# Four of eight samples' value pages summed on GpSimd instead of TensorE, in one layer of a hybrid decoder

## The chip, the cores and the metric

The kernel runs on one core of a Trainium2 chip. The metric is the device time of one execution in microseconds, taken as the median over runs. A core has TensorE (PE, matrix products into PSUM), VectorE (DVE), ScalarE (ACT) and GpSimd (POOL) for elementwise work, and SyncE (SP), which here only starts DMAs. The engines run side by side, each through its own list of instructions in order, and wait for each other at semaphores.

## What is computed

One layer of a decoder, for 256 tokens of a prompt and 8 samples with one new token each: a normalised input goes through one wide projection, then through an attention branch and a Mamba-2 (SSD) branch, both gated, merged, projected, and followed by a gated FFN. Cut to what matters here:

```python
h = rmsnorm(x, norm_mix_pre)
q, k, v, z, xbc, dt_raw, g_attn, g_ssm = split(h @ w_in)
attn = moba_attention(q, k_all, v_all, q_pos0)    # prompt: own keys; a sample: 1024 past keys and values
ssm, conv_new, ssm_new = mamba2_branch(z, xbc, dt_raw, ...)
merged = sigmoid(g_attn) * (attn @ w_attn_out) + sigmoid(g_ssm) * (ssm @ w_ssm_out)
x = x + rmsnorm(merged @ w_out, norm_mix_post)
x = x + rmsnorm(swiglu(rmsnorm(x, norm_ffn_pre), w_gate, w_up, w_down), norm_ffn_post)

# attention of one sample, for each of 16 heads of 64 numbers; p is 0 in the blocks left out
p = softmax(q . k_past / 8 over the chosen 3 of 4 blocks, and the own key)
out = sum over 1024 positions of p * v_past, + p_own * v
```

The past keys and values lie in pages of 128 positions x 1024 numbers (512 KB), found by a page table: eight pages of keys and eight of values for each sample.

## The kernel before

All is fp32. Weights are split into a high part (w_hi, made by ScalarE's `hi_half`) and the rest (w_lo, made by VectorE's `lo_half`: raw minus w_hi), and each product is taken as three fast ones. The work is cut into 562 *blocks*: one block is 128 output columns by up to eight 128-row slices of a weight, 24 matmuls on TensorE over all 264 tokens. w_hi lies in a ring of four, so ScalarE and VectorE can be up to three blocks ahead of TensorE. The blocks come in the fixed order of `pairs`: projection (blocks 0 to 209), SSM output (210 to 241), attention output (242 to 257), and so on.

All other work stands beside the blocks by hand. Each engine runs `for b in range(END)`: its share of block b, and then `side_work(b)`, in which tables of block numbers say what is due. SyncE starts what stands at b when TensorE begins block b (`wait(sp, mm_done, b)`), and its list is in order too. ScalarE issues the weight loads.

The samples' attention has two parts. *Keys* (block 30 on, `K_AT`): SyncE loads a page of keys into one of four slots of `kv`, GpSimd multiplies it with the query (line 744), VectorE sums over each head (line 1401). After the softmax (`SEL`, done at block 150; GpSimd's list then holds only `ends`), *values* (`V_AT`, blocks 152 to 232): for each of four pairs of samples there are eight steps, one page of each of the two samples at a time, two blocks apart (`VG[w] + 2 g`). A step (lines 2017 to 2029) is four fp32 products of 32 columns of probabilities with half a page, each in two passes, side by side in four column groups of TensorE; all heads are multiplied with all columns, and the eight steps add up in the PSUM bank `side[3]`. VectorE then keeps each head's own columns (`vm_done`, line 1461), TensorE adds these up (the *pair sum*, line 2034, four products in two passes each), and VectorE adds the own token into `attn` (line 1468). A step uses two of the four slots and its loads are issued four blocks ahead.

In the same blocks the SSD groups run (`SSD`: a group every eleven blocks; GpSimd's `ends` makes its `xw`, which TensorE needs at `SSD[g] + 6` and + 7; TensorE writes `y` to `side[0]` at + 10), the old states of the samples are read (`STATE`; `st`, `stx`, `crows`), and `u` is normalised (`UN`, blocks 196 to 214). ScalarE writes the gates `gate_a`, 16 tiles of 264 columns, from `ga` pairs, the last four pairs at blocks 201 to 213. `side[0]` and `side[2]` are PSUM banks that these share.

## Time and profile before

| | us |
|---|---|
| median of 3 runs | 1783.56 (1782.84 to 1790.49) |
| profiled execution, its own time | 1781.87 |
| its span | 1780.1 |
| TensorE busy | 1756.1 |
| VectorE busy | 1193.5 |
| ScalarE busy | 912.5 |
| GpSimd busy | 221.1 |

TensorE's granted clock is full (1.00) in all the stretches that are spoken of here. "Busy" is the time in which an engine works on an instruction; where it is held up inside an instruction by another engine, that counts as busy too, and the instruction's duration grows. A matmul row shows a duration of about 0.28 us, but matmuls overlap: what one costs is the distance between the starts of neighbours.

In the value stage the trace finds these starts of value steps: block 152 at 519.8 us, 174 at 603.3, 188 at 657.5, 196 at 685.4, 210 at 740.4, 218 at 766.1, 232 at 815.1.

### The profile page before, as it was taken

To read this page: it belongs to the slowest core of one execution; us is meant where nothing else is said; L and a number is where in the kernel's file an instruction comes from. 1 tells how busy PE (TensorE), PEld (TensorE's weight loads), DVE (VectorE), ACT (ScalarE), POOL (GpSimd) and SP (SyncE) were. 2 spreads that over 40 slices of the span, in tenths; PEclk is the share of its full clock that TensorE was granted. 3 is DMA by queue.
4 is the path that set the end of the run, shared out by engine and by line. 5 is a ranking of instruction groups with operands and counts; after the bars stand their busy time and mean duration, and the time that the engine had idled before them with its cause. 6 is when DMAs were issued, how large, how long until landed. Compare 5 with 4: busy or idle time off the path is not lost.

```text
span 1780.1 us, 35190 instructions
## 1 busy us (share of the span) xinstructions
PE 1756.1 (99%) x14510; PEld 1708.2 (96%) x14510; DVE 1193.5 (67%) x1679; ACT 912.5 (51%) x1724; POOL 221.1 (12%) x127
## 2 busy tenths in 40 slices
PE   8999999999999999999999999999999999999997
PEld 7999999999988988889999999999999999999997
DVE  6468999999887656845755666666666666444444
ACT  5544556555766556533454655554555454434442
POOL 2144645564000000000000000000000000000000
PEclk9999999999999999999999999999999999999999
DMA  8589988897789999695565487777777776655553
GB/s 256 174 271 332 321 269 275 281 305 243 229 266 338 291 306 328 223 304 189 186 222 182 134 276 228 223 227 234 219 226 235 217 235 202 215 177 189 164 181 97
DMA packets 398272, 421.39 MB, mean 237 GB/s; under 512 B 13040, under 2 KB 375984, under 8 KB 397072
## 3 DMA queue, kind: packets, MB, share of 16 engines
q10 hardware_dynamic: 284480, 285.62, 49.9%
q1 hardware_dynamic: 113280, 132.85, 23.0%
q8 instruction: 114, 1.87, 0.4%
q0 software_dynamic: 352, 0.67, 0.2%
q14 instruction: 46, 0.38, 0.1%
HBM read 400.70 MB, written 18.66 MB: 236 GB/s over the span
## 4 chain that ended last, share of the span: by engine, by line
PE 91%; DVE 6%; DMA 1%; ACT 1%; SPq 0%; issue 0%; DVEq 0%; ACTq 0%
PE gemm L1770 29%; PE gemm L1771 28%; PE gemm L1772 28%; DVE w_lo L1204 2%; PE side L2026 2%; PE side L1732 1%; DVE sc_flat L1401 1%; DMA kv<-in_cache_v 1%; DMA xtok<-in_x_prompt 1%; DVE u L1196 0%; DVE conv_out L1196 0%; DVE un L1524 0%; ACT w_hi L774 0%; DVE dec L1193 0%; PE side L1922 0%
## 5 line engine op out<-in xcount | busy, mean ns | idle before, releaser
L1204 DVE TENSOR_TENSOR w_lo<-raw,w_hi 128x1024 fp32r<-128x1024 f32 (+1 forms) x562 | 737.9, 1317 | 538.6 <-ACT w_hi L774 537.7
L1770 PE MATMUL gemm<-x_hi,w_hi 128*128 128x264 f32 x3312 | 951.7, 287 | 3.7 <-DVE x_lo L1532 1.9
L1772 PE MATMUL gemm<-x_hi,w_lo 128*128 128x264 f32 x3312 | 938.2, 283 | 0.0
L1771 PE MATMUL gemm<-x_lo,w_hi 128*128 128x264 f32 x3312 | 937.9, 283 | 0.0
L774 ACT ACTIVATE w_hi<-raw 128x1024 fp32r<-128x1024 f32 (+1 forms) x562 | 585.6, 1044 | 655.3 <-PE gemm L1772 654.8
L1770 PEld LDWEIGHTS gemm<-x_hi,w_hi 128*128 128x128 f32 x3312 | 623.6, 188 | 30.9 <-issue 24.1
L1771 PEld LDWEIGHTS gemm<-x_lo,w_hi 128*128 128x128 f32 x3312 | 624.4, 189 | 0.9 <-issue 0.5
L1772 PEld LDWEIGHTS gemm<-x_hi,w_lo 128*128 128x128 f32 x3312 | 621.1, 188 | 0.0
L744 POOL TENSOR_TENSOR kv<-kv,qb 128x1024 f32<-128x1024 f32 x64 | 180.6, 2830 | 176.4 <-DMA kv<-in_cache_k 176.3
L1771 PE MATMUL gemm<-g_lo,w_hi 128*128 128x264 f32 x704 | 200.4, 285 | 0.0
L1770 PE MATMUL gemm<-g_hi,w_hi 128*128 128x264 f32 x704 | 199.9, 284 | 0.0
L1772 PE MATMUL gemm<-g_hi,w_lo 128*128 128x264 f32 x704 | 199.6, 284 | 0.0
L1770 PEld LDWEIGHTS gemm<-g_hi,w_hi 128*128 128x128 f32 x704 | 132.6, 188 | 0.0
L1772 PEld LDWEIGHTS gemm<-g_hi,w_lo 128*128 128x128 f32 x704 | 132.6, 188 | 0.0
L1771 PEld LDWEIGHTS gemm<-g_lo,w_hi 128*128 128x128 f32 x704 | 132.2, 188 | 0.0
L1401 DVE TENSOR_REDUCE sc_flat<-kv 128x16 f32<-128x1024 f32 x64 | 77.2, 1207 | 2.3 <-POOL kv L744 2.3
L1770 PE MATMUL gemm<-m_hi,w_hi 128*128 128x264 f32 x256 | 73.3, 286 | 0.0
L1771 PE MATMUL gemm<-m_lo,w_hi 128*128 128x264 f32 x256 | 72.5, 283 | 0.0
L1772 PE MATMUL gemm<-m_hi,w_lo 128*128 128x264 f32 x256 | 72.5, 283 | 0.0
L774 ACT ACTIVATE stx<-stx 128x128 f32<-128x128 f32 x128 | 37.8, 299 | 31.1 <-DVE stx L1193 31.1
L1770 PEld LDWEIGHTS gemm<-m_hi,w_hi 128*128 128x128 f32 x256 | 48.2, 188 | 0.1
L1771 PEld LDWEIGHTS gemm<-m_lo,w_hi 128*128 128x128 f32 x256 | 48.3, 189 | 0.0
(324 smaller groups left out, 1391.9 us busy)
## 6 DMA issues: line engine op xcount, KB each, us to landing
raw<-in_w_in ACTq DMA_DIRECT2D x99, 1024.0 KB, 7.3
raw<-in_w_gate ACTq DMA_DIRECT2D x44, 1024.0 KB, 5.2
raw<-in_w_up ACTq DMA_DIRECT2D x44, 1024.0 KB, 5.7
raw<-in_w_down ACTq DMA_DIRECT2D x40, 1024.0 KB, 5.4
kv<-in_cache_k SPq DMA_DIRECT2D x64, 512.0 KB, 5.8
kv<-in_cache_v SPq DMA_DIRECT2D x64, 512.0 KB, 6.1
st<-in_state_ssm SPq DMA_DIRECT2D x64, 256.0 KB, 5.5
raw<-in_w_ssm_out ACTq DMA_DIRECT2D x16, 1024.0 KB, 7.3
```

Of the source, the lines that this page charges most:

```text
L744: gp.tensor_tensor(out=page_slot(m), in0=page_slot(m), in1=qb[:, n % 2, :], op=ALU.mult)\
L774: return nc.scalar.activation(out, in_, f, **kw)
L1204: v.tensor_tensor(w_lo[:, s, 0:blk.kts, cols], raw[:, s, 0:blk.kts, cols], w_hi[:, b % RING, 0:blk.kts].bitcast(fp32), ALU.subtract).then_ ...
L1401: v.tensor_reduce(out=sc[:, g, n, :], in_=by_head(page_slot(m)), axis=AX.X, op=ALU.add)\
L1732: return nc.tensor.transpose(out, in_, ident[0:k, 0:k])
L1770: mm(out, w_hi[:, b % RING, k], pr.hi[:, x], start=(x == 0), stop=False)
L1771: mm(out, w_hi[:, b % RING, k], pr.lo[:, x], start=False, stop=False)
L1772: ins = mm(out, w_lo[:, s, k, cols], pr.hi[:, x], start=False, stop=(x == pr.kt - 1))
L2026: ins = mm(side[3][32 * n:32 * n + 32, :], sc_flat[:, first_col:first_col + 32], page_slot(2 * m + e)[:, half * 512:(half + 1) * 512], sta ...
```

## The change

Samples 0 to 3 (two pairs) stay with TensorE, in steps that are now four blocks apart (`VE`: 153 to 181, and 188 to 216) and use slots 0 and 1 alone. Samples 4 to 7 go to GpSimd: every two blocks from 149 to 211 (`PV_AT`) SyncE loads one value page into slot 2 or 3, and two blocks later GpSimd multiplies it in place with its probabilities, spread over each head's 64 columns, and adds it to `vsum`; a sample's first page is multiplied straight into `vsum`. For each sample TensorE then sums `vsum` over the 128 positions by eight products with a column of ones (the *page sum*, `PV_SUM`: blocks 174, 186, 211 and 221, in `side[0]` or `side[2]`), and VectorE adds the own token. `vsum` takes the place of gate tiles 8 to 15, which are now written over the old states' buffers (`gate_b`, `gate_c`), once all 32 state multiplications are done. GpSimd's `ends` stand three blocks earlier. The load of the page table is counted with the other small vectors (`vecs_in` for `pages_in`, left out below). Where `v_cp` was waited for up to 4 it is now 6, or the count of the sum whose bank is used next (left out too, but for one).

```diff
@@ -165,6 +165,9 @@
+        gate_b = at("gate_b", [P, 7, T], fp32, T0)
+        gate_c = at("gate_c", [P, T], fp32, T0 + 9984)
+        vsum = at("vsum", [P, 2, AW], fp32, G0 + 8704)
...
-        VG = [152 + 22 * w for w in range(4)]
+        VE = [[153 + 4 * g for g in range(NPG)], [188 + 4 * g for g in range(NPG)]]
+        PV_AT = [149 + 2 * q for q in range(4 * NPG)]
+        PV_SUM = [174, 186, 211, 221]
+        PAIR_NTH, SUM_NTH = [2, 5], [1, 3, 4, 6]
+        V_ALL = 6
-        V_AT = [VG[w] + 2 * g for w in range(4) for g in range(NPG)]
+        V_AT = [x for two in VE for x in two]
...
+        def pooled_page(q):
+            return kv[:, 2 + q % 2, :]
+        def gate_a_of(t):
+            return gate_a[:, t, :] if t < 8 else gate_b[:, t - 8, :] if t < 15 else gate_c[:, :]
+        def sum_psum(j):
+            return side[(0, 0, 2, 0)[j]][:, 0:2 * AT]
...
-                for m in range(4 * NPG):
-                    if b != V_AT[m] - 4:
+                for m in range(2 * NPG):
+                    if b != V_AT[m] - 3:
-                    if m == 0:
-                        sp.wait_ge(k_red, NB * NPG)
-                    wait(sp, v_mm, m - 1)
-                    if g < 2:
-                        wait(sp, vs_mm, w)
+                    wait(sp, v_mm, m)
+                    if g == 0:
+                        wait(sp, vs_mm, PAIR_NTH[0] if w else 0)
-                        sp.dma_start(page_slot(2 * m + e), src).then_inc(kv_in[m % 2], 16)
+                        sp.dma_start(kv[:, e, :], src).then_inc(kv_in[0], 16)
+            def pooled_loads(b):
+                for q in range(4 * NPG):
+                    if b != PV_AT[q]:
+                        continue
+                    if q == 0:
+                        sp.wait_ge(k_red, NB * NPG)
+                    wait(sp, pg_add, q - 1)
+                    src = vc[bass.ds(page_of(4 + q // NPG, q % NPG), 1)].rearrange("g p n -> p (g n)")
+                    sp.dma_start(pooled_page(q), src).then_inc(kv_in[2 + q % 2], 16)
...
-                    if d == 5:
+                    if d == 2:
...
-                    if d == 6:
+                    if d == 3:
+            def pooled_values(b):
+                for q in range(4 * NPG):
+                    if b != PV_AT[q] + 2:
+                        continue
+                    j, g = q // NPG, q % NPG
+                    page, total = pooled_page(q), vsum[:, j % 2, :]
+                    share = sc[:, g, 4 + j, :].unsqueeze(2).to_broadcast([P, HEADS, HD])
+                    if q == 0:
+                        gp.wait_ge(p_done, 1)
+                    if g == 0 and j >= 2:
+                        gp.wait_ge(vs_mm, SUM_NTH[j - 2])
+                    gp.wait_ge(kv_in[2 + q % 2], 256 + 16 * (q // 2 + 1))
+                    if g == 0:
+                        gp.tensor_tensor(out=by_head(total), in0=by_head(page), in1=share, op=ALU.mult)\
+                            .then_inc(pg_add, 1)
+                    else:
+                        drained(gp.tensor_tensor(out=by_head(page), in0=by_head(page), in1=share, op=ALU.mult))
+                        gp.wait_ge(pg_add, q)
+                        gp.tensor_tensor(out=total, in0=total, in1=page, op=ALU.add).then_inc(pg_add, 1)
+                pooled_values(b)
...
-                        func(gate_a[:, t, :], ps[:, 0:T], ACT.Tanh, scale=0.5).then_inc(free_out[par], 1)
+                        if t >= 8:
+                            act.wait_ge(st_mul, 4 * NB)
+                        func(gate_a_of(t), ps[:, 0:T], ACT.Tanh, scale=0.5).then_inc(free_out[par], 1)
...
-                for w in range(4):
-                    if b == VG[w] + 18:
+                for w in range(2):
+                    if b == VE[w][-1] + 4:
-                        mul(by_head(kv[:, 2, 0:512]), by_head(side[3][:, :]), own).then_inc(vm_done, 1)
-                    if b == VG[w] + 21:
-                        dve.wait_ge(vs_mm, w + 1)
+                        mul(by_head(kv[:, 0, 0:512]), by_head(side[3][:, :]), own).then_inc(vm_done, 1)
+                    if b == VE[w][-1] + 7:
+                        dve.wait_ge(vs_mm, PAIR_NTH[w])
...
+                for j in range(4):
+                    if b == PV_SUM[j] + 4:
+                        dve.wait_ge(vs_mm, SUM_NTH[j])
+                        n = 4 + j
+                        v.tensor_tensor(attn[:, :, TP + n], sum_psum(j)[:, 0:2 * AT:2],
+                                        own_t[:, n * AT:(n + 1) * AT], ALU.add).then_inc(v_cp, 1)
...
+                        for j in range(2):
+                            if PV_SUM[j] < b <= PV_SUM[j] + 11:
+                                pe.wait_ge(v_cp, SUM_NTH[j])
...
-                for m in range(4 * NPG):
+                for m in range(2 * NPG):
-                        wait(pe, v_cp, w)
-                    pe.wait_ge(kv_in[m % 2], 256 + 32 * (m // 2 + 1))
+                        wait(pe, v_cp, PAIR_NTH[0] if w else 0)
+                    pe.wait_ge(kv_in[0], 256 + 32 * (m + 1))
-                                 page_slot(2 * m + e)[:, half * 512:(half + 1) * 512],
+                                 kv[:, e, half * 512:(half + 1) * 512],
-                for w in range(4):
-                    if b == VG[w] + 17:
+                for w in range(2):
+                    if b == VE[w][-1] + 3:
-                            ins = mm(side[3][:, 4 * k:4 * k + 4], kv[:, 2, k * P:(k + 1) * P], bsel[:, :],
+                            ins = mm(side[3][:, 4 * k:4 * k + 4], kv[:, 0, k * P:(k + 1) * P], bsel[:, :],
+                                     start=True, stop=True)
+                        ins.then_inc(vs_mm, 1)
+                for j in range(4):
+                    if b == PV_SUM[j]:
+                        pe.wait_ge(pg_add, NPG * (j + 1))
+                        if j < 2:
+                            pe.wait_ge(y_done, 6 + j)
+                        if j == 2:
+                            pe.wait_ge(un_sd, 6)
+                        if j == 3:
+                            pe.wait_ge(ct_cp, 3)
+                        for t in range(AT):
+                            ins = mm(sum_psum(j)[:, 2 * t:2 * t + 2], vsum[:, j % 2, t * P:(t + 1) * P], ones[:, 0:2],
...
```


The order of GpSimd's list, where the SSD groups 6 and 7 lay alone (blocks 176 to 188); each three rows are one group's `xw`:

```order
L756 TENSOR_TENSOR xw_86<-xdt,dend 128x256
L759 TENSOR_TENSOR xw<-xw_86,cdec 128x256
L764 TENSOR_TENSOR xw_86<-xdt,dend 128x256
L756 TENSOR_TENSOR xw_86<-xdt,dend 128x256
L759 TENSOR_TENSOR xw<-xw_86,cdec 128x256
L764 TENSOR_TENSOR xw_86<-xdt,dend 128x256
L58 UNCONDITIONAL_BRANCH
```

The same engine now, from block 171 to block 175:

```order
L812 TENSOR_TENSOR kv<-kv,sc_flat 128x1024
L814 TENSOR_TENSOR vsum<-vsum,kv 128x1024
L784 TENSOR_TENSOR xw_86<-xdt,dend 128x256
L787 TENSOR_TENSOR xw<-xw_86,cdec 128x256
L812 TENSOR_TENSOR kv<-kv,sc_flat 128x1024
L814 TENSOR_TENSOR vsum<-vsum,kv 128x1024
L792 TENSOR_TENSOR xw_86<-xdt,dend 128x256
L812 TENSOR_TENSOR kv<-kv,sc_flat 128x1024
L814 TENSOR_TENSOR vsum<-vsum,kv 128x1024
```

Two large operations for a page now stand before, between and behind those of a group.

TensorE's side work in blocks 152 to 158, without the large matmuls between the rows (first before, then now); `kv,sc_flat` is a value step, the others belong to an SSD group:

```order
L2026 MATMUL side<-kv,sc_flat 32x512 x4
...
L2026 MATMUL side<-kv,sc_flat 32x512 x4
...
L1960 MATMUL side<-bct 128x128 x2
L1961 MATMUL side<-xw_86,btok 128x256
...
L1966 MATMUL side<-btok,xw 128x128
L1967 MATMUL side<-btok,xw_86 128x128
L1966 MATMUL side<-btok,xw 128x128
L1967 MATMUL side<-btok,xw_86 128x128
L2026 MATMUL side<-kv,sc_flat 32x512 x4
...
L2026 MATMUL side<-kv,sc_flat 32x512 x4
```

```order
L2087 MATMUL side<-kv,sc_flat 32x512 x4
...
L2018 MATMUL side<-bct 128x128 x2
L2019 MATMUL side<-xw_86,btok 128x256
...
L2024 MATMUL side<-btok,xw 128x128
L2025 MATMUL side<-btok,xw_86 128x128
L2024 MATMUL side<-btok,xw 128x128
L2025 MATMUL side<-btok,xw_86 128x128
...
L2087 MATMUL side<-kv,sc_flat 32x512 x4
```

Four steps have become two, the rest keeps its place.

## Rows read from the trace of the kernel before

**Rows 1.** The page: busy time by engine, and the chain's shares.
```profile
PE 1756.1 (99%) x14510; PEld 1708.2 (96%) x14510; DVE 1193.5 (67%) x1679; ACT 912.5 (51%) x1724; POOL 221.1 (12%) x127
...
PE 91%; DVE 6%; DMA 1%; ACT 1%; SPq 0%; issue 0%; DVEq 0%; ACTq 0%
```

**Rows 2.** Waits of TensorE, whole run: us, times, longest.
```profile
PE gemm L1770 <- DVE x_lo L1532: 1.9, 2, 1.2
...
PE side L2026 <- DMA kv<-in_cache_v: 0.5, 1, 0.5
```

**Rows 3.** Timeline of TensorE around one value step: start, duration.
```profile
772.89 0.28 PE L1772 MATMUL gemm<-x_hi,w_lo 128*128 128x264 f32 x1
773.10 1.06 PE L2026 MATMUL side<-kv,sc_flat 128*32 128x512 f32 x8
774.09 0.39 PE L1770 MATMUL gemm<-x_hi,w_hi 128*128 128x264 f32 x1
774.32 0.28 PE L1771 MATMUL gemm<-x_lo,w_hi 128*128 128x264 f32 x1
```

**Rows 4.** Timeline of TensorE around one pair sum.
```profile
585.17 0.28 PE L1772 MATMUL gemm<-x_hi,w_lo 128*128 128x264 f32 x1
585.29 0.95 PE L2034 MATMUL side<-bsel,kv 128*128 128x4 f32 x8
586.09 0.37 PE L1770 MATMUL gemm<-x_hi,w_hi 128*128 128x264 f32 x1
586.30 0.28 PE L1771 MATMUL gemm<-x_lo,w_hi 128*128 128x264 f32 x1
```

**Rows 5.** Windows: stretch, length, busy PE, PEld, DVE, ACT, POOL, clock, DMA.
```profile
100.00:440.00 340.00, 338.92 (x2857) 331.33 (x2857) 317.30 (x360) 182.82 (x374) 188.06 (x70) 1.00 0.89 292
514.00:758.00 244.00, 241.59 (x1979) 215.42 (x1978) 165.78 (x274) 152.80 (x408) 10.97 (x12) 1.00 0.92 303
```

**Rows 6.** GpSimd's line 744, durations in ns: min/median/max.
```profile
L744 POOL TENSOR_TENSOR kv<-kv,qb x64: 2377/2586/3739, 102.7 to 430.6; 128x1024 f32<-128x1024 f32 x64
```

**Rows 7.** Timeline of GpSimd, 400 to 405 us.
```profile
400.23 0.61 POOL L759 TENSOR_TENSOR xw<-xw,cdec 128x256 f32<-128x256 f32 x1
400.80 2.41 POOL L744 TENSOR_TENSOR kv<-kv,qb 128x1024 f32<-128x1024 f32 x1
403.16 1.60 POOL L764 TENSOR_TENSOR xw<-xdt,dend 128x256 f32<-128x256 f32 x1
```

**Rows 8.** Timeline of VectorE at the same time.
```profile
401.06 3.23 DVE L1204 TENSOR_TENSOR w_lo<-raw,w_hi 128x1024 fp32r<-128x1024 f32 x1
```

**Rows 9.** Groups of VectorE, 100 to 440 us: busy us, mean ns.
```profile
L1204 DVE TENSOR_TENSOR w_lo<-raw,w_hi 128x1024 fp32r<-128x1024 f32 x103 | 184.2, 1797 | 21.8 <-ACT w_hi L774 21.5
L1401 DVE TENSOR_REDUCE sc_flat<-kv 128x16 f32<-128x1024 f32 x63 | 76.0, 1207 | 2.3 <-POOL kv L744 2.3
```

**Rows 10.** Groups of VectorE, 514 to 758 us.
```profile
L1204 DVE TENSOR_TENSOR w_lo<-raw,w_hi 128x1024 fp32r<-128x1024 f32 x66 | 81.1, 1229 | 75.2 <-ACT w_hi L774 75.2
L1193 DVE TENSOR_TENSOR stx<-st,crows 128x512 f32<-128x512 f32 x22 | 15.0, 684 | 0.0
...
L1196 DVE SCALAR_TENSOR_TENSOR u<-u,gains,un 128x264 f32<-128x264 f32 x16 | 7.2, 491 | 0.3
L1532 DVE TENSOR_TENSOR x_lo<-u,x_hi 128x264 fp32r<-128x264 f32 x16 | 5.8, 425 | 0.0
L1193 DVE TENSOR_TENSOR dec<-dec,cbm 128x512 f32<-128x512 f32 x8 | 5.2, 688 | 0.1
...
L1196 DVE SCALAR_TENSOR_TENSOR u<-tmp,u 128x256 f32<-128x256 f32 x10 | 4.2, 418 | 0.0
...
L1510 DVE TENSOR_TENSOR ysam<-ysam,both_t 128x32 f32<-128x32 f32 x3 | 0.6, 192 | 0.1
```

**Rows 11.** DMA issues, 514 to 758 us: KB each, median us to landing.
```profile
kv<-in_cache_v SPq DMA_DIRECT2D x48, 512.0 KB, 6.3
...
crows<-bc_row SPq DMA_DIRECT2D x20, 128.0 KB, 9.5
```

More of the change, by code:

```diff
@@ L638, in side_work @@
                 key_loads(b)
+                pooled_loads(b)
                 value_loads(b)
@@ L875, in time_steps @@
                 if b == DT + 2:
-                    act.wait_ge(vecs_in, 48)
+                    act.wait_ge(vecs_in, 64)
                     p = at_pair["dt", 0]
@@ L1034, in attn_halves @@
                 if b == B_AO - 2:
-                    act.wait_ge(v_cp, 4)
+                    act.wait_ge(v_cp, V_ALL)
                     act.wait_ge(u_lo, KT)
@@ L1627, in evac @@
                         t = 2 * i + n
-                        gate = gate_s if pr.kind == "so" else gate_a
+                        gate = gate_s[:, t, :] if pr.kind == "so" else gate_a_of(t)
                         if t == 0 and pr.kind == "so":
@@ L1631, in evac @@
                         dve.wait_ge(mm_done, last_of[p][n] + 1)
-                        stt(gate[:, t, :], gate[:, t, :], 1.0, gemm_ps[2 * par + n][:, 0:T], ALU.add, ALU.mult)\
+                        stt(gate, gate, 1.0, gemm_ps[2 * par + n][:, 0:T], ALU.add, ALU.mult)\
                             .then_inc(free_out[par], 1)
@@ L1637, in evac @@
                         dve.wait_ge(free_out[par], freed(p) - 1 + n)
-                        v.tensor_tensor(gate_s[:, t, :], gate_s[:, t, :], gate_a[:, t, :], ALU.add).then_inc(ao_sum, 1)
+                        v.tensor_tensor(gate_s[:, t, :], gate_s[:, t, :], gate_a_of(t), ALU.add).then_inc(ao_sum, 1)
                     for n in range(2):
@@ L2043, in u_norm @@
                         pe.wait_ge(fin_cp, NG)
+                        pe.wait_ge(v_cp, SUM_NTH[1])
                         wait(pe, un_sd, g - 2)
@@ L2051, in conv_tails @@
                     pe.wait_ge(un_sd, NG)
+                    pe.wait_ge(v_cp, SUM_NTH[2])
                     pe.wait_ge(xbc_done, CT)
@@ L2063, in token_sums @@
                     pe.wait_ge(ct_cp, 3)
-                    pe.wait_ge(v_cp, 4)
+                    pe.wait_ge(v_cp, V_ALL)
                 if i == 7:
```

16 lines of the change are left out of this document (8 added, 8 removed).

## The prediction

> **What bounds the kernel now.** I read the engine shares and the chain of waits first. TensorE is busy 99% of the span and 91% of the chain is its own work [rows 1]; what it waits for is small, 1.9 us for VectorE's x_lo and 0.5 us for a value page [rows 2]. So a pass taken off TensorE is worth its whole time, as long as the engine behind it keeps up. Every block (one 128-column weight tile over eight 128-row slices, 24 matmuls 0.12 us apart, 2.9 us) needs a w_lo from VectorE. Second, I read VectorE where GpSimd also works. In the key stage (100 to 440 us) VectorE is busy 317 of 340 us with GpSimd at 188, in the value stage (514 to 758 us) 166 of 244 with GpSimd at 11 [rows 5]. That stretch is blocks 151 to 215, over which the change spreads its GpSimd pages.
>
> **What the change takes off TensorE.** A value step (eight passes over two pages) is read against the matmuls around it: from the last before it to the second after it 1.43 us [rows 3], where two steps of 0.12 would stand, so 1.19 us. It drops 16 of 32: 19.0 us. A pair sum is 585.17 to 586.30 less the same two steps, 0.89 us [rows 4], and two of four go: 1.8 us. The one wait for a page, 0.5 us, goes with it [rows 2]. Added are four page sums, each 8 fp32 products of 128x128 weights with 2 columns, so 16 passes. The trace has no such row; the nearest is the pair sum, same weights, 4 columns, 8 passes in 0.80 us, so 0.89 + 0.80 = 1.69 us each, 6.8 in all. Bounds: 4.4 for all if only the 0.12 us between large matmuls and half as many passes counted, 9 if each needed 0.14. TensorE's own balance: -19.0 - 1.8 - 0.5 + 6.8 = **-14.5 us**, of which -7.9 lies in blocks 151 to 215 (24 steps become 15, three pair sums become one, three page sums come) and -6.6 behind (8 steps become 1, one page sum comes). This needs nothing else to become late.
>
> **What it puts on GpSimd.** 32 pages: four start a sum (one multiply), 28 take a multiply and an add, so 60 operations of 128x1024. The nearest row is the key multiply: 2.38 us at its least, 2.59 in the median [rows 6]. The broadcast operand costs nothing extra by the 128x256 xw row with one, 0.61 us for a quarter of the size [rows 7]. I take 2.39 where nothing holds it: 143 us, and with the twelve xw operations already there (12 x 0.61 = 7) 151 us, to go into a stretch that TensorE would now pass in 244 - 7.9 = 236 us. Alone it fits.
>
> **What it does to VectorE.** This is the step that decides. The w_lo subtraction takes 1.23 us in the mean of the value stage but 1.80 in the key stage, while the reduction of a page, which has one input, keeps 1.21 there [rows 9, 10]. The timeline says why: w_lo started at 401.06, GpSimd's multiply ran from 400.80 to 403.21, and w_lo ended at 404.29, 1.08 us after it; GpSimd's xw of 403.16 then took 1.60 for 0.61, ending 0.61 after w_lo's end at about 404.2. So the two take turns, whole instructions at a time [rows 7, 8]. Instructions with one SBUF input (the reduction, the steps that read PSUM) run beside GpSimd.
>
> The Trainium skill says the same in "SBUF — State Buffer", section "SBUF: two separate sides": the port pair is an exclusive lock, kept for the instruction by whichever starts first, against a VectorE instruction with two SBUF inputs, and the other blocks fully. The trace agrees, with the 3.23 us w_lo above. If the two merely shared bandwidth, this change would keep its gain.
>
> So in blocks 151 to 215 turns must add up. VectorE's two-input work there is w_lo 81.1, stx 15.0, u 7.2, x_lo 5.8, dec 5.2, and 17 of smaller forms, u from tmp (4.2) the largest and ysam (0.6) among the last [rows 10]: 132 us in 176 instructions, less about 0.08 us each by which a row overlaps the next, 118 us. With GpSimd's 151 that is 269 us of turns for 236 us of TensorE. Key stage, same count: 64 x 2.39 + 4 = 157 and, with some 14 for the smaller forms, 103 x 1.13 + 14 = 130, 287 of 340, which fitted, and TensorE lost 1 us there [rows 5]. The value stage would be at 114%.
>
> Ends of the cost, for that stretch against today's 244 us:
> - least: turns packed without a gap, less the lead of two blocks (2 x 2.9 = 6 us) that the weight ring allows: 263, +19. If GpSimd may also finish as late as its last sum (block 221) instead of 215, six more blocks (17 us of TensorE for some 8 us of VectorE's turns) relieve it by up to 9: +10.
> - most: nothing of VectorE beside GpSimd: 166 + 151 - 6 = 311, +67.
> - by the key stage: GpSimd's 157 us there cost VectorE about 103 x 0.57 = 59 on w_lo and, as an estimate in the ratio 14 to 116 of the turns, 9 more on the smaller forms, 68 in all, so 89 ran beside the 142 us (340 - 68 - 130) in which VectorE was idle or on one-input work, 62%. Here that is 166 - 118 = 48 us, 30 of it covered: 166 + 151 - 30 - 6 = 281, +37.
> I take +28, the middle of +19 and +37, and with the -6.6 behind the stretch **+21 us**. The saving inside the stretch is then worth nothing, since w_lo and not TensorE sets the pace.
>
> **The moved and added waits.** SyncE issues page q at block 149 + 2q, behind a wait for page q - 2's add; queued behind it are the state rows, the decay rows and TensorE's pages. A page lands in 6.3 us and the state's crows take 9.5 [rows 11]. A slot's round is 6.3 + 1.5 to issue + two operations with one turn of VectorE each, 7 or so, 15 us for four blocks; four blocks are 14 us at TensorE's pace and 16 at the slower one, so SyncE runs at most a block late. The last V loads come three blocks ahead instead of four and no longer wait for the step just before: cost nothing, 0.5 per step if late. xw stands three blocks earlier in GpSimd's list, where it blocks the pages until VectorE's xdt is there: it delays a page by about a block, covered by the slack of sum 0 (page 7 done at block 167, used at 174), less so for sum 1 (183, used at 186). A late sum 1 costs up to 8 us; I put 0 in. The last gate tiles wait for the last state multiply, one block before them on VectorE; ScalarE is two blocks ahead: nothing, 2 us if VectorE lags. The merged semaphore costs nothing, since all four small loads are long done.
>
> **Sum.** The profiled execution took 1781.87 us, span 1780.1 and 1.8 around it. 1781.9 + 21 = **1803 us**. It lies 1.7 below the median of the runs, 1783.56, well inside their spread.
>
> **Rivals.**
> 1. *Absorbed by slack, faster.* VectorE is idle in 78 of 244 us of the value stage, and in the key stage it took 93% load with TensorE losing 1 us [rows 5]. If the turns cost only 68/157 of GpSimd's time as there, VectorE needs 166 + 65 = 231 of 236 us and nothing waits: 1781.9 - 14.5 = 1767. Against it: the 86 us of GpSimd that would have to run beside VectorE's one-input and idle time find only 48 + 5.
> 2. *GpSimd is the one that gives way.* Turns go mostly to VectorE and pages pile up to the last sum at block 221. Then the least case holds with +10 - 6.6: 1785. Against it: SyncE would be held behind page adds, and state rows with it.
> 3. *Queue jam.* GpSimd falls over a block behind, SyncE stands in a page's wait, crows and V pages come late, and TensorE waits for the sums as well. From +37, plus 8 for sum 1 and some 10 for late rows: 1830. This decides from a page round of over four blocks (16 us).
>
> **Chances.** Main case 0.58 (own range 1790 to 1818), rival 1 0.17, rival 2 0.15, rival 3 0.10. A measurement here tells about 0.5%, 9 us, from no change. Faster: rival 1 and a little, 0.19. Same: most of rival 2 and the foot of the main case, 0.20. Slower: 0.61. The range leaves most of rival 1 outside below and the far part of the most-case above: 1774 to 1832.
>
> **What would show it.** Right: w_lo's mean in blocks 151 to 215 rises to 1.8 us or more with its median of other stages unchanged, and TensorE's waits in the stretch are for w_lo, some 25 to 35 us. The stretch of the value stage grows, the stages behind 830 us keep their length. Page sums show 16 passes in about 1.7 us. Wrong: TensorE as full as today there and the span 14 us shorter (rival 1); waits of TensorE on vsum or kv instead of w_lo (rivals 2, 3); GpSimd's page operations far off 2.4 to 3.2 us each.

## The result, and the profile after

| | before | after |
|---|---|---|
| median, us (lowest to highest) | 1786.78 (1782.84 to 1790.49) | 1822.88 (1819.80 to 1829.95) |
| profiled execution / its span | 1781.87 / 1780.1 | 1829.95 / 1828.4 |

The ratio is 1.0203, with a 95% interval of 1.0181 to 1.0224. The change makes the kernel 36 us slower. The forecast was 1803, 16 above the same median, with a range that ended at 1832: the direction came out and so did the turns of the two engines, the size did not.

First the page of the changed kernel, against [rows 1]: busy time by engine, then VectorE's, GpSimd's and the granted clock's lines over 40 equal slices.

```profile
PE 1765.4 (97%) x14430; PEld 1728.8 (95%) x14430; DVE 1305.0 (71%) x1677; ACT 909.4 (50%) x1724; POOL 365.5 (20%) x187
...
DVE  6468999999899999974665666666666666444444
...
POOL 2155544455027576420000000000000000000000
PEclk8999999999999999889999999999999999999999
```

TensorE has 80 matmuls fewer and is busy for 9 us *more*. That can't come from waiting; it is the first sign of something that the prediction left out. VectorE has two instructions fewer and is busy for 111 us more.

The windows of TensorE locate it. Columns: stretch, length, busy (instructions), granted clock, DMA share, GB/s. The four stretches are the start, up to block 149 (the own token's scores, `own_p`), blocks 149 to 214 (the transposes of `tails`), and the rest. Before:

```profile
0.00:370.00 370.00, 362.30 (x3007) 1.00 0.85 274
370.00:510.60 140.60, 138.33 (x1171) 1.00 0.78 242
510.60:754.00 243.40, 240.96 (x1973) 1.00 0.92 301
754.00:1780.00 1026.00, 1014.52 (x8365) 1.00 0.65 207
```

After, at the same places of the program:

```profile
0.00:370.00 370.00, 362.70 (x2985) 0.99 0.83 271
370.00:524.80 154.80, 146.72 (x1194) 0.96 0.74 225
524.80:809.00 284.20, 248.10 (x1934) 0.93 0.86 285
809.00:1828.40 1019.40, 1007.93 (x8324) 1.00 0.63 201
```

So the 48.3 us between the two profiled spans (12 more than between the medians, for the profiled execution of the changed kernel is its longest, and that of the kernel before is among its shortest) divide like this:

| stretch | length | idle TensorE (length less busy) | busy TensorE |
|---|---|---|---|
| up to block 149 | +14.2 | +5.4 | +8.8 |
| blocks 149 to 214 | +40.8 | +33.7 | +7.1 (39 matmuls fewer, clock 0.93 for 1.00) |
| behind | -6.6 | 0.0 | -6.6 |

The third row is the -6.6 us that was forecast for it. The second was put at +28, the first at nothing. What TensorE waits for (us in total, times, longest), against [rows 2]:

```profile
PE gemm L1828 <- DVE w_lo L1256: 18.4, 11, 5.2
PE gemm L1828 <- DVE x_lo L1590: 9.4, 1, 9.4
PE side L2121 <- DVE u_sq L1579: 8.7, 4, 5.0
PE side L2087 <- DMA kv<-in_cache_v: 4.8, 3, 3.1
...
PE side L2039 <- DVE dec L1245: 2.6, 2, 1.6
```

All but the pages' 4.8 us is VectorE being late. Its groups from 514 to 758 us, against [rows 10]: busy us, mean ns of one.

```profile
L1256 DVE TENSOR_TENSOR w_lo<-raw,w_hi 128x1024 fp32r<-128x1024 f32 x58 | 102.6, 1773 | 12.3 <-ACT w_hi L824 12.3
L1245 DVE TENSOR_TENSOR stx<-st,crows 128x512 f32<-128x512 f32 x24 | 32.1, 1336 | 0.0
L1680 DVE COPY zs<-tmp 128x8 f32<-128x8 f32 x12 | 14.5, 1206 | 0.4
...
L1582 DVE RECIPROCAL un<-un 128x264 f32<-128x264 f32 x3 | 5.4, 1791 | 0.0
...
L1248 DVE SCALAR_TENSOR_TENSOR u<-tmp,u 128x256 f32<-128x256 f32 x12 | 5.0, 414 | 0.0
```

w_lo goes from 1229 to 1773 ns and stx from 684 to 1336. The reciprocal keeps its time (1795 before), and so do the forms that read PSUM. `u<-tmp,u` has two inputs in SBUF and keeps 414 ns all the same; it stands right behind the copy `zs` in VectorE's list, and the copy does the waiting, as e5 shows below. `zs` copies 8 columns and has a single input, and yet goes from 172 to 1206 ns. Before:

```profile
L1622 DVE COPY zs<-tmp 128x8 f32<-128x8 f32 x10 | 1.7, 172 | 0.3
```

The timelines around 741 us show the turns, in VectorE (start, duration) and then GpSimd:

```profile
741.22 3.55 DVE L1248 SCALAR_TENSOR_TENSOR u<-u,gains,un 128x264 f32<-128x264 f32 x2
744.69 2.12 DVE L1579 TENSOR_TENSOR u_sq<-u_sq 128x264 f32<-128x264 f32 x1
746.74 3.38 DVE L1256 TENSOR_TENSOR w_lo<-raw,w_hi 128x1024 fp32r<-128x1024 f32 x1
```

```profile
740.08 1.91 POOL L812 TENSOR_TENSOR kv<-kv,sc_flat 128x1024 f32<-128x1024 f32 x1 [10.59 <-DMA kv<-in_cache_v]
742.07 2.41 POOL L814 TENSOR_TENSOR vsum<-vsum,kv 128x1024 f32<-128x1024 f32 x1
744.44 2.09 POOL L812 TENSOR_TENSOR kv<-kv,sc_flat 128x1024 f32<-128x1024 f32 x1
746.61 2.42 POOL L814 TENSOR_TENSOR vsum<-vsum,kv 128x1024 f32<-128x1024 f32 x1
```

A small `u_sq` of 0.43 us takes 2.12 and ends 0.28 us behind GpSimd's multiply (746.81 and 746.53); w_lo of 1.23 takes 3.38 and ends 1.09 us behind the add. Note the 10.59 us: GpSimd stood without a page, then two pages had landed, and four long operations followed without a gap. TensorE's wait of 4.97 us for `u_sq` ends at 747, inside this burst. Whether such bursts matter beyond the average was not tried: no run spaced the same pages more evenly.

### The profile page after: what moved, and what is told of

It reads as the page before. It is cut to its first block, busy times and chain, and to the rows that moved or that the text cites. A ratio compares the mean times of both kernels' runs of the same rounds, so it can differ in the third digit from the quotient of the medians.

```text
span 1828.4 us, 35123 instructions
## 1 busy us (share of the span) xinstructions
PE 1765.4 (97%) x14430; PEld 1728.8 (95%) x14430; DVE 1305.0 (71%) x1677; ACT 909.4 (50%) x1724; POOL 365.5 (20%) x187
## 4 chain that ended last, share of the span: by engine, by line
PE 70%; DVE 21%; issue 4%; ACT 4%; POOL 0%; DMA 0%; ACTq 0%; DVEq 0%; SPq 0%; POOLq 0%
PE gemm L1828 23%; PE gemm L1829 22%; PE gemm L1830 22%; DVE w_lo L1256 8%; DVE u L1248 2%; DVE sc_flat L1453 2%; DVE conv_out L1248 2%; ACT w_hi L824 2%; DVE stx L1245 1%; PE side L1790 1%; ACT stx L824 1%; DVE un L1582 1%; DVE zs L1680 1%; DVE bct L1248 1%; DVE att_st L1359 0%
## 5 line engine op out<-in xcount | busy, mean ns | idle before, releaser
L1256 DVE TENSOR_TENSOR w_lo<-raw,w_hi 128x1024 fp32r<-128x1024 f32 (+1 forms) x562 | 766.3, 1368 | 474.0 <-ACT w_hi L824 473.4
L1828 PEld LDWEIGHTS gemm<-x_hi,w_hi 128*128 128x128 f32 x3312 | 631.7, 191 | 46.2 <-issue 31.9
L1829 PEld LDWEIGHTS gemm<-x_lo,w_hi 128*128 128x128 f32 x3312 | 632.2, 191 | 1.0 <-issue 0.5
L1830 PEld LDWEIGHTS gemm<-x_hi,w_lo 128*128 128x128 f32 x3312 | 628.6, 190 | 0.0
L772 POOL TENSOR_TENSOR kv<-kv,qb 128x1024 f32<-128x1024 f32 x64 | 176.3, 2767 | 175.7 <-DMA kv<-in_cache_k 175.5
L812 POOL TENSOR_TENSOR kv<-kv,sc_flat 128x1024 f32<-128x1024 f32 x28 | 61.5, 2196 | 86.6 <-DMA kv<-in_cache_v 86.6
L814 POOL TENSOR_TENSOR vsum<-vsum,kv 128x1024 f32<-128x1024 f32 x28 | 76.1, 2717 | 2.2
```

Of the source, the lines that this page charges most:

```text
L772: gp.tensor_tensor(out=page_slot(m), in0=page_slot(m), in1=qb[:, n % 2, :], op=ALU.mult)\
L812: drained(gp.tensor_tensor(out=by_head(page), in0=by_head(page), in1=share, op=ALU.mult))
L814: gp.tensor_tensor(out=total, in0=total, in1=page, op=ALU.add).then_inc(pg_add, 1)
L1256: v.tensor_tensor(w_lo[:, s, 0:blk.kts, cols], raw[:, s, 0:blk.kts, cols], w_hi[:, b % RING, 0:blk.kts].bitcast(fp32), ALU.subtract).then_ ...
L1828: mm(out, w_hi[:, b % RING, k], pr.hi[:, x], start=(x == 0), stop=False)
L1829: mm(out, w_hi[:, b % RING, k], pr.lo[:, x], start=False, stop=False)
```

## The experiments

| run | median, us | ratio to before (95%) |
|---|---|---|
| e1_ends_late | 1816.75 | 1.0171 (1.0137 to 1.0205) |
| e2_before_ends_early | 1792.3 | 1.0032 (1.0016 to 1.0047) |
| e3_tiny_pages | 1780.64 | 0.9963 (0.9941 to 0.9985) |
| e4_multiplies_only | 1780.44 | 0.9970 (0.9954 to 0.9986) |
| e5_zs_from_psum | 1817.36 | 1.0170 (1.0151 to 1.0189) |
| e6_memsets | 1783.15 | 0.9972 (0.9955 to 0.9990) |
| e7_two_samples | 1802.53 | 1.0084 (1.0066 to 1.0103) |
| e9_quarter_turns | 1812.78 | 1.0131 (1.0114 to 1.0148) |
| e10_first_two_full | 1791.69 | 1.0028 (1.0014 to 1.0043) |
| e11_last_two_full | 1798.42 | 1.0068 (1.0042 to 1.0094) |
| e12_two_samples_early | 1786.88 | 1.0002 (0.9983 to 1.0021) |
| e13_pauses | 1843.87 | 1.0310 (1.0288 to 1.0332) |
| e14_short_pauses | 1796.5 | 1.0054 (1.0033 to 1.0075) |

Each ratio is to executions of the kernel before taken beside the run, with medians of 1785.4 to 1788.4. e5's median leaves out one of its four executions, of 1907.32 us at a granted clock of 0.845 for 0.987 to 0.989 in the others. "Stretch" below is blocks 149 to 214, 243.4 us before and 284.2 after.

### The xw that was moved up

e1_ends_late is the changed kernel with `ends` where it was:

```diff
-                    if d == 2:
+                    if d == 5:
-                    if d == 3:
+                    if d == 6:
```

> The changed kernel with GpSimd's xw operations of an SSD group put back to 5 and 6 blocks behind the group's start, as before. In the changed kernel's trace the own-score product of block 149 starts at 524.8 us against 510.6 before, 14.2 us late ahead of any value page, and GpSimd stands 12.9 us in front of an xw while key pages pile up. Theory M (the earlier xw holds the key pages): that part comes back, about 12 us, 1808 to 1814. Rival (the 14 us are chance, or come from something else): 1820 to 1826.

e2_before_ends_early is the kernel before with the opposite edit and nothing else.

> The kernel before with only GpSimd's xw operations moved three blocks earlier (2 and 3 blocks behind a group's start). Theory M: 8 to 15 us slower than the kernel before, the own-score product of block 149 at 518 to 526 us instead of 510.6. Rival: within 3 us of the kernel before.

Measured: putting the move into the kernel before costs 0.32%, 5.7 us (3 to 8 by the interval); taking it out of the changed kernel brings 6.1 us by the medians, though there the intervals of the two ratios overlap. So the move seems to cost some 6 us, less than the 8 to 15 and the 12 that were expected. The figure is not firm: e14 below has xw at its old place, and is some 10 us slower than before, of which its pauses explain 5.9.

Block 149 is reached at 520.8 us in e2 and 510.6 before, at 524.8 after and 513.7 in e1. A single execution's mark is a weak witness, for kernels with late xw reach it anywhere from 510.6 (before) to 519.3 us (e14). Much of that spread goes with the first microseconds. Where the granted clock over 10 to 30 us is 0.91 (before) or 0.83 to 0.84 (e1, e5, e7, e11, e12, e13), the mark is at 510.6 to 513.7; where it is 0.74 it is at 514.3 to 519.3 with late xw (e3, e4, e6, e9, e10, e14), and at 520.8 and 524.8 in e2 and the changed kernel, whose clock there is 0.74 too. So of the 14.2 us between the two profiled executions only 5.5 to 10.5 lie beyond what late xw shows after such a start, and of e2's 10.2 only 1.5 to 6.5.

How the move costs is seen in GpSimd's list in the changed kernel, where no value page is worked yet:

```profile
408.94 1.47 POOL L784 TENSOR_TENSOR xw<-xdt,dend 128x256 f32<-128x256 f32 x1 [12.88 <-issue]
...
413.99 10.87 POOL L772 TENSOR_TENSOR kv<-kv,qb 128x1024 f32<-128x1024 f32 x4
```

It waits 12.9 us at xw until VectorE's `xdt` is there (408.39). Four *key* pages pile up behind it and are then worked in a row. (e2 shows the same: 13.48 us at xw, then four pages in a row.) VectorE meanwhile, at w_lo again:

```profile
414.62 2.84 DVE L1256 TENSOR_TENSOR w_lo<-raw,w_hi 128x1024 fp32r<-128x1024 f32 x1
...
417.84 1.91 DVE L1680 COPY zs<-tmp 128x8 f32<-128x8 f32 x1
...
422.59 3.36 DVE L1256 TENSOR_TENSOR w_lo<-raw,w_hi 128x1024 fp32r<-128x1024 f32 x1
```

TensorE then waits 4.52 us for w_lo, at 426 us; in e2 it is 4.51. Late xw can have a wait there too, but a shorter one (1.89 to 2.87 us in e3, e4, e9, e10 and e14).

### Is it the size of GpSimd's operations, or their number and waits?

e3_tiny_pages leaves every DMA, wait and semaphore of e1, but 56 of the 60 page operations work on 64 of 1024 columns (part of the computation left out).

```diff
-    drained(gp.tensor_tensor(out=by_head(page), in0=by_head(page), in1=share, op=ALU.mult))
+    drained(gp.tensor_tensor(out=by_head(page)[:, 0:1], in0=by_head(page)[:, 0:1], in1=share[:, 0:1], op=ALU.mult))
-    gp.tensor_tensor(out=total, in0=total, in1=page, op=ALU.add).then_inc(pg_add, 1)
+    gp.tensor_tensor(out=total[:, 0:64], in0=total[:, 0:64], in1=page[:, 0:64], op=ALU.add).then_inc(pg_add, 1)
```

> As e1, but of the 60 page operations of GpSimd only the four that start a sum are whole; the other 56 work on 64 of 1024 columns (so samples 4 to 7 lack most of their sum). All loads, waits and sums of TensorE stay. Theory L (VectorE and GpSimd take turns, and the turns of 60 operations do not fit): the saving of TensorE shows, 14.5 us below the kernel before, 1768 to 1773. Rival Q (SyncE's list, the page loads or the two slots hold the work up): stays within 10 us of e1.

Measured 1780.6, 36 us under e1 and 0.37% (6.6 us) under before: the whole loss is the work of GpSimd. It is not the 1768 to 1773 that was expected. This kernel also shows what TensorE alone gains. Its busy time in the stretch is 235.8 us (240.96 before) and 1008.0 behind (1014.5): 11.7 us, where 14.5 were counted. About half of it comes through; the rest goes to small waits (6.2 us for w_lo, 2.4 for x_lo, 2.3 for pages).

e4_multiplies_only keeps the 32 multiplies at full size and drops the 28 adds (part of the computation left out).

```diff
-    drained(gp.tensor_tensor(out=by_head(page), in0=by_head(page), in1=share, op=ALU.mult))
-    gp.wait_ge(pg_add, q)
-    gp.tensor_tensor(out=total, in0=total, in1=page, op=ALU.add).then_inc(pg_add, 1)
+    gp.tensor_tensor(out=by_head(page), in0=by_head(page), in1=share, op=ALU.mult).then_inc(pg_add, 1)
```

> As e1, but GpSimd only multiplies its 32 pages and adds none (samples 4 to 7 get their first page alone). Turns in blocks 151 to 215 fall to 118 + 7 + 32 x 2.39 = 201 us for TensorE's 236. Theory L with a threshold: nearly as fast as e3, 1770 to 1778. Rival (each GpSimd operation costs its share whatever the load, so 32 of 60 cost 53%): half way between e3 and e1, about 1790.

Measured 1780.4 (1770 to 1778 was expected), the same as with hardly any work, though w_lo's mean is 1389 ns and not 1229. So 32 operations in 64 blocks cost nothing and 60 cost 36 us. The price is not proportional; it is what is left over when VectorE's slack is used up.

### Is it reading SBUF, or GpSimd's being busy?

e6_memsets puts four memsets of 128x1024 in the place of each page's operations, two for a sample's first page (the sums are left out). GpSimd writes twice as much, and reads nothing.

```diff
+    wait(gp, pg_add, q)
+    for _ in range(3 if g else 1):
+        drained(gp.memset(total, 0.5))
+    gp.memset(total, 0.5).then_inc(pg_add, 1)
```

> As e1, but each page's operations on GpSimd are replaced by four memsets of 128x1024 (two for a sample's first page), which write SBUF and read nothing (so samples 4 to 7 get no past values). By the rows 128x128 takes 0.205 us, so 1.0 to 1.6 us each, 4 to 6 us a page, about as long as before. Theory L in the form that only GpSimd's reading conflicts: w_lo back to 1.23 us, 1772 to 1784. Rival (any long GpSimd instruction holds VectorE, or GpSimd's lateness in itself delays the kernel): 1805 to 1820 like e1.

```profile
L810 POOL MEMSET vsum<- 128x1024 f32 x88 | 84.0, 955 | 137.3 <-DMA kv<-in_cache_v 133.8
L811 POOL MEMSET vsum<- 128x1024 f32 x32 | 30.5, 953 | 1.8
```

```profile
L1253 DVE TENSOR_TENSOR w_lo<-raw,w_hi 128x1024 fp32r<-128x1024 f32 x68 | 83.6, 1231 | 74.2 <-ACT w_hi L821 74.2
L1242 DVE TENSOR_TENSOR stx<-st,crows 128x512 f32<-128x512 f32 x23 | 15.7, 682 | 0.0
...
L1677 DVE COPY zs<-tmp 128x8 f32<-128x8 f32 x10 | 6.1, 607 | 0.4
```

With 114.5 us of GpSimd's time in the stretch, w_lo and stx are as before to 2 ns, and the time is 1783. Of GpSimd's two kinds of work only the one that reads SBUF holds up VectorE's two-input work. The copy `zs` is another matter: it is late even behind a memset (607 ns). The Trainium skill ("SBUF — State Buffer", section "SBUF: two separate sides") names two cases: a VectorE instruction with two SBUF inputs, against a GpSimd instruction that reads SBUF; and one in a two-port mode, against any. w_lo agrees with the first, at 1231 ns beside memsets and 1773 beside page operations. The copy fits the second, if it runs in such a mode, which no trace here shows.

e5_zs_from_psum is e1 with `zs` computed from PSUM, to price that second case.

```diff
+    stt(zs[:, t, :], sq[:, n, TP:T], 1.0, gemm_ps[2 * par + n][:, TP:T], ALU.add, ALU.mult)
-    v.tensor_copy(zs[:, t, :], tmp[:, n, TP:T])
```

> As e1 (GpSimd's xw late again), and VectorE's small copy of 128x8 into zs, 1.21 us in the mean of the changed kernel's value stage against 0.17 before, is made from PSUM instead, by a step with one SBUF input. Theory L, widened (a plain fp32 copy from SBUF to SBUF takes a turn too): the copies fall to about 0.2 us, VectorE gains 10 to 12 us there and the kernel 6 to 12 us against e1, 1805 to 1811. Rival (the copy is slow for another reason, or VectorE does not set the pace): within 3 us of e1.

`zs` falls to 152 ns, and the time is that of e1 (1817.4 and 1816.8): a miss for the expectation. The turn is now waited for by the next instruction on VectorE that has two SBUF inputs. It is `u<-tmp,u`, which goes from 415 ns in e1 to 1198:

```profile
L1248 DVE SCALAR_TENSOR_TENSOR u<-tmp,u 128x256 f32<-128x256 f32 x10 | 12.0, 1198 | 0.3
```

Behind GpSimd's operation one of the two has to wait, so taking the copy away saves nothing.

### Is the length of a turn what hurts?

e9_quarter_turns is e1 with each page operation cut in four of 128x256.

```diff
+    parts = [slice(4 * k, 4 * k + 4) for k in range(4)]
+    for hs in parts:
+        ins = gp.tensor_tensor(out=by_head(page)[:, hs], in0=by_head(page)[:, hs], in1=share[:, hs], op=ALU.mult)
...
+    for hs in parts:
+        ins = gp.tensor_tensor(out=by_head(total)[:, hs], in0=by_head(total)[:, hs], in1=by_head(page)[:, hs], op=ALU.add)
```

> As e1, but each of the 60 page operations is cut into four of 128x256, so GpSimd gives its turn up after some 0.6 us instead of 2.4. Theory L by the sum of turns: the sum is the same, 240 small turns of 0.61 (147 us), so 1812 to 1820, or up to 8 us more for gaps. Rival H (it is the length of one hold-up that starves w_lo, not the sum): 1790 to 1805.

w_lo falls from 1781 to 1474 ns, but GpSimd's busy time in 514 to 758 us grows from 152 to 207. It takes 1812.8, 4 us less than e1, with intervals that overlap, and inside the 1812 to 1820 of the sum of turns. TensorE's waits change their owner:

```profile
PE side L2025 <- POOL xw L784: 9.3, 2, 7.5
PE gemm L1835 <- DVE x_lo L1597: 7.9, 2, 6.5
PE side L2031 <- POOL xw L792: 6.2, 2, 4.4
PE gemm L1835 <- DVE w_lo L1263: 4.6, 5, 2.9
```

I read this as both engines together having more to do than the stretch holds, with shorter turns only choosing which is late. But the cut also added those 55 us of GpSimd's time, so the run does not show what shorter turns alone would do.

### Where in the stretch does it cost?

e10_first_two_full works samples 4 and 5 (blocks 151 to 182) at full size and the others on 64 columns; e11_last_two_full is the mirror (part of the computation left out in both).

```diff
+    n_h = HEADS if j < 2 else 1        # e11: if j >= 2
+    n_c = AW if j < 2 else 64
```

> The version with late xw (ends at blocks 5 and 6), but only the pages of samples 4 and 5 (blocks 151 to 182) are worked at full size; of the pages of samples 6 and 7 the multiply and the add take 64 of 1024 columns (part of the computation left out). With all pages small it took 1780.6, with all large 1816.8: 36 us for 60 operations. Theory of turns: what costs is where GpSimd's turns meet VectorE's own two-input work. In blocks 151 to 183 VectorE has w_lo (37 us) and the smaller forms (8), so 45 + 75 us of turns against 116 of TensorE: barely over. Expected 1786 to 1792, and TensorE's waits in 514:620 us under 6 us. Rival, cost per page wherever it stands: half of 36, so 1799.

> The mirror of the run before: samples 6 and 7 at full size (blocks 183 to 214), samples 4 and 5 small (part of the computation left out). In these blocks VectorE has w_lo (37 us), the smaller forms (8) and the normalisation of u (some 25 to 30 us of two-input work): 72 + 75 = 147 us of turns against 116. Expected 1804 to 1812, with TensorE's waits on u_sq and x_lo. Rival, cost per page wherever it stands: 1799. If both halves alone cost under 10 us each, the cost is one of piling up over the whole stretch, and neither of the two.

Over e3 the first half alone costs 11 us, the second 18, both together 36. e10's time is in its range, but TensorE waits 12.3 us in 514 to 620 us, where under 6 was expected. The second half is the dearer one, and its waits are those of the changed kernel (x_lo 9.2 us, u_sq 8.4, and 4.6 for a page), but the expectation had 24 to 31 us for it. The two parts lack 7 us of the whole; that pages of the first half also leave less slack for the second is a guess. And 30 operations in one half cost 11 or 18 us where e4's 32, spread over both, cost nothing: what counts is how densely they stand, not only how many there are.

### Fewer pages on GpSimd

e7_two_samples gives GpSimd only samples 6 and 7, a page every four blocks, and TensorE three pairs every three blocks (with xw late and `zs` from PSUM).

```diff
-        VE = [[153 + 4 * g for g in range(NPG)], [188 + 4 * g for g in range(NPG)]]
-        PV_AT = [149 + 2 * q for q in range(4 * NPG)]
-        PV_SUM = [174, 186, 211, 221]
+        VE = [[153 + 29 * w + 3 * g for g in range(NPG)] for w in range(3)]
+        PV_AT = [149 + 4 * q for q in range(2 * NPG)]
+        PV_SUM = [186, 221]
-                    if b != V_AT[m] - 3:
+                    if b != V_AT[m] - 2:
```

> A version meant to be faster than both: only samples 6 and 7 on GpSimd, a page every four blocks (30 operations instead of 60), three pairs on TensorE in steps three blocks apart (153, 182, 211 on), xw late, zs from PSUM. TensorE saves 8 steps (9.5 us) and one pair sum (0.9) for two page sums (3.4): 7 us. Theory L: turns in the value stage are 118 + 7 + 30 x 2.39 = 197 us for 240, so nothing waits for them and it is 7 us below the kernel before, 1776 to 1782. Rival (each operation costs its share, 30 of 60 of the 48 us that e1 lost against its saving): about 1800.

Measured 1802.5. The trace names one cause: TensorE's pages were loaded two blocks ahead, and it waited 10.4 us for them, 7 times. e12_two_samples_early mends that, and also ends GpSimd's pages before `u` is normalised, so that what each of the two brings stays open:

```diff
-        PV_AT = [149 + 4 * q for q in range(2 * NPG)]
+        PV_AT = [149 + 3 * q for q in range(2 * NPG)]
-                    if b != V_AT[m] - 2:
+                    if b != V_AT[m] - 3:
```

> Two samples' pages on GpSimd instead of four, now every three blocks (149 to 194, so that they end before the normalisation of u), three pairs on TensorE every three blocks with their loads issued three blocks ahead instead of two. TensorE's own saving over before: 8 steps of 1.19 and one pair sum of 0.89 less two page sums of 1.69, 7 us. The run with every fourth block and loads two ahead took 1802.5, with 10.4 us of waits for value pages and a granted clock of 0.96. Theory (those waits and the meeting with the normalisation are the cost): page waits under 3 us, 1776 to 1784, the fastest version or equal to before. Rival (30 operations in 45 blocks still take turns that VectorE needs): 1790 to 1800, w_lo about 1.5 us in 514:650.

1786.9, no difference from before (1.0002), and above the 1776 to 1784 that was expected. Page waits are 1.4 us and the stretch takes 242.4 us. Of the 7 us that TensorE was to save, 4.9 show as shorter busy time in the stretch and behind it; 3.4 us more of idle time in the stretch (x_lo alone 3.5 us) take most of that again. No version that I ran with true page sums beats the kernel before.

### What a wait of TensorE costs beyond itself

e13_pauses is the kernel before with six pauses in the FFN's first product, where TensorE has no gap and GpSimd nothing to do.

```diff
+    PAUSE = {B_FF + 40 + 25 * i: n for i, n in enumerate((8, 14, 22, 32, 44, 60))}
+    # GpSimd, at block b of PAUSE
+    gp.wait_ge(mm_done, b + 1)
+    for _ in range(PAUSE[b] - 1):
+        drained(gp.memset(conv_k[:, :, :], 0.5))
+    gp.memset(conv_k[:, :, :], 0.5).then_inc(xw_done, 1)
+    # TensorE, behind block b
+    pe.wait_ge(xw_done, 3 * NG + sorted(PAUSE).index(b) + 1)
```

> The kernel before, and in the stage of the feed-forward's first product, where TensorE is busy without a gap and GpSimd does nothing, six pauses: GpSimd waits for the end of a block's product, does 8, 14, 22, 32, 44 and 60 small memsets, and TensorE waits for that; 25 blocks (72 us) between them. Nothing else waits long. It measures what a wait of TensorE costs beyond its own length. Theory: after a pause of a few us TensorE works on at a lower granted clock for a while, so the kernel's stretch between two pauses grows by more than the pause, by 0.2 to 0.6 us for each us of the longer ones (in the changed kernel 33.7 us more of idle time came with 12.4 us more of busy time). Rival: the granted clock stays 1.00 behind them, and the span grows by the sum of the pauses alone.

TensorE's windows around the first pause, which is its shortest (2.15 us, ending at 1121.64):

```profile
1010.00:1119.00 109.00, 108.65 (x900) 1.00 0.75 238
...
1122.00:1132.00 10.00, 10.00 (x72) 0.83 0.47 142
1132.00:1142.00 10.00, 10.00 (x85) 1.00 0.61 188
```

```profile
1123.00:1124.00 1.00, 1.00 (x6) 0.50 0.06 18
...
1125.00:1126.00 1.00, 1.00 (x8) 0.73 0.00 0
1126.00:1127.00 1.00, 1.00 (x10) 1.00 0.00 0
```

Behind the pause the clock is at its lower level, 0.50 or 1.2 GHz, and then at 2.4 GHz again. "Busy" is 10 us of 10 in both of the longer windows, but one holds 72 matmuls and the other 85: 13 at 0.12 us, so 1.5 us are lost with no idle time to show for it. The same count gives 1.5 us behind the pause of 3.7 us (72 matmuls), 2.8 and 2.7 behind those of 5.8 and 15.8 (61 and 62), 1.9 and 1.8 behind those of 8.4 and 11.6 (69 and 70). The distances agree: 25 blocks take 72.6 us in this stage of the kernel before, and from one pause's start to the next it is 76.5, 78.0, 81.4, 83.0 and 85.8 us, which leaves 1.6 to 3.0 us beside the pause itself. So the clock does fall, as the theory had it, but the extra cost is one per pause and hardly depends on its length.

e14_short_pauses has 1 to 6 memsets in place of 8 to 60.

> The run with pauses again, with 1 to 6 small memsets each, so that TensorE waits some 0.4 to 1.6 us at the six places. In the run before, the pause of 2.15 us was followed by a granted clock of 0.50 for some microseconds and 1.5 us of lost time. Theory: the fall follows an idle time of any such length, so the windows of 10 us behind each pause show a clock under 1.00 and about 1.5 us are lost at each. Rival: the short ones leave the clock at 1.00 and the distance between neighbouring pauses is the 72.6 us of 25 blocks plus the pause; the fall begins somewhere between 0.4 and 2.15 us, and the rows show at which of the six.

All six stay at 1.00, and no window of 10 us from 1110 to 1550 shows less. The last and longest:

```profile
1493.50 1.25 POOL L775 MEMSET conv_k<- 128x128 f32 x5 [72.88 <-PE gemm L1779]
```

The 72.88 us are the 72.6 of 25 blocks and 0.3 more: nothing was lost behind the pause ahead of it. In these two runs pauses of up to 1.6 us were not followed by a fall; the one of 2.15 was. e14 as a whole is 1.0054 of before, some 10 us, and the six pauses sum to 5.9; in the profiled execution most of the rest lies ahead of them (block 149 at 519.3 us), where nothing was edited. In the changed kernel it goes the same way. From 370 to 809 us TensorE has twelve waits of 1.6 us or less and eight longer ones, of 3.01, 4.52, 3.47, 5.15, 3.06, 4.97, 2.24 and 9.36 us, and the clock falls behind those eight alone. One of them:

```profile
746.96 1.22 PE L2121 MATMUL side<-u_sq,ones 128*128 128x264 f32 x2 [4.97 <-DVE u_sq L1579]
...
750.00:760.00 10.00, 9.71 (x68) 0.86 0.18 49
```

The other runs blur the border. A wait of 2.86 us in e14 itself (first pair of rows) is not followed by a fall, and one of 1.85 us in e9 (second pair) is:

```profile
419.81 0.36 PE L1777 MATMUL gemm<-x_hi,w_hi 128*128 128x264 f32 x1 [2.86 <-DVE w_lo L1211]
...
419.80:429.80 10.00, 9.99 (x83) 1.00 0.65 187
```

```profile
638.97 0.46 PE L2025 MATMUL side<-bct 128*128 128x128 f32 x2 [1.85 <-POOL xw L784]
...
639.00:649.00 10.00, 10.00 (x67) 0.83 0.88 293
```

The longest wait without a fall is 3.51 us (e5, ending at 704.3); behind the first 30 us every longer one in the traces has a fall behind it. And in e1 and e11 the clock falls at 620 and 611 us right behind a page sum, 16 narrow passes, with no wait of TensorE in the ten microseconds ahead. So the length of a single wait does not decide alone between 1.8 and 3.5 us.

## Why the prediction failed

Its steps, one by one.

- *TensorE's own balance, -14.5.* e3, with the same steps, shows -5.2 in the stretch for -7.9, and -6.5 behind for -6.6. The page sum was priced at 1.69 us and takes 1.81 (from its start at 629.87 to the next block's at 631.68). Right within 3 us.
- *GpSimd's operations at 2.39 us.* Right: in 514 to 758 us the two kinds take 2.49 in the mean, with their waiting for turns. The multiply with its spread operand is the cheaper one.

```profile
L814 POOL TENSOR_TENSOR vsum<-vsum,kv 128x1024 f32<-128x1024 f32 x24 | 66.4, 2767 | 1.9
L812 POOL TENSOR_TENSOR kv<-kv,sc_flat 128x1024 f32<-128x1024 f32 x24 | 53.1, 2212 | 56.5 <-DMA kv<-in_cache_v 56.5
```

- *Turns, whole instructions at a time.* Right, and shown from both sides: memsets of about the same time on GpSimd leave w_lo at 1231 ns (e6), page operations put it at 1773. The forecast said 1.8 or more. It also said that TensorE's waits would be for w_lo, 25 to 35 us; VectorE makes it wait 30.4 us in the stretch, but only 9.7 for w_lo, for with a late w_lo everything behind it on VectorE is late too (x_lo 9.4, u_sq 8.7, dec 2.6).
- *+28 us for the stretch.* This term failed; it measured +40.8. It was VectorE's lateness, with TensorE's saving of 7.9 already used up in it: 28 + 7.9 = 35.9 us of waits, and TensorE is idle for 36.1 us of the stretch. The waiting was sized right. What is missing is that TensorE works slower behind it. Its busy time in the stretch is 248.1 us where e3 needs 235.8 for the same work, 12.3 us more, in six falls of the clock to 1.2 GHz at some 2 us each, as e13 prices them. e1 repeats it: 248.0 us busy in the stretch. I wrote "TensorE's pace" with a single clock in mind, because every row of before shows 1.00, and took a microsecond of waiting to cost a microsecond. (The lead was taken as two blocks; the ring of four allows three, which makes each end of the sum 3 us smaller and explains nothing of the miss.)
- *xw three blocks earlier, priced at nothing.* This failed too. I asked which value pages stand behind xw in GpSimd's list, and did not ask for key pages, though SSD groups 0 to 3 run while keys are still worked. e1 and e2 put it at about 6 us of the median, with the doubt that e14 leaves. In the profiled execution the part up to block 149 grew by 14.2 us. The waits for w_lo of 3.01 and 4.52 us at 388 and 426 us lie in it, with a fall of the clock behind each. Some 3 us more were lost at the start, where the clock over 10 to 30 us is 0.74 against 0.91 before: at 370 us TensorE is 22 matmuls behind. That part belongs to the execution and not to the change: e14, which has the lists of the kernel before up to there, shows 0.74 too.
- *Instructions with one SBUF input run beside GpSimd.* True of the reciprocal (1791 ns for about as much before), false of the copy (172 to 1206 ns). It cost nothing, since the next instruction would have waited in its place (e5).
- *The queues: SyncE's wait, value loads three blocks ahead.* GpSimd lacks pages for 56.5 us in 514 to 758 (the row above), and TensorE waits 4.8 us for its own. "At most a block late" was too kind, but as a price it is 4 us, and those waits too bring a fall of the clock (3.06 us, at 719).
- *Rivals.* Absorbed by slack: it holds for 32 operations spread over the stretch (e4), not for 60. GpSimd gives way: no, its pages are late, but TensorE waits for VectorE. Queue jam: its time of 1830 is the nearest to the result, its cause is not what was found.

Put together by medians: 21 in the forecast, some 6 for the earlier xw, and 9 of the 12 of the clock give 36. That last figure is a remainder and not a measurement: the profiled execution is 7 us above its median, and the falls of the clock differ between executions.

## What to carry to other kernels

Where GpSimd gets work that reads SBUF, add its time to VectorE's two-input time over the stretch and ask that the sum leaves room: here half of the work was free when it was spread evenly, and cost 11 to 18 us when it was packed into half of the stretch; all of it cost 36 us. Then price the waits of TensorE that remain not by their length alone: here the single ones of under 1.8 us cost only themselves, each of over 3.5 us some 2 us more, and between the two it went either way. When an instruction that can wait is moved up an in-order list, look at everything behind it over the whole run, not only at what the change itself adds.

## What the runs showed of the chip that was not expected

- TensorE's clock can fall to 1.2 GHz behind a single idle time of 1.85 or 2.15 us within a stage that is otherwise full; in other places 2.86 and 3.51 us were not followed by a fall. It costs 1.5 to 2.8 us each time, for pauses from 2 to 16 us alike. The idle row doesn't show it: TensorE counts as busy.
- GpSimd's memset (955 ns for 128x1024) does not delay VectorE's w_lo and stx, which have two SBUF inputs (1231 and 682 ns with it, 1229 and 684 without), but it does delay a small fp32 copy from SBUF to SBUF (172 to 607 ns).
- Cutting GpSimd's operations in four does not give the time back: four quarters of an add took 4 x 1051 ns beside VectorE, a whole one 2767.
